# A reordered start of a second projection: the first two row tiles share the first column half, and two zeroings are moved

## The chip, the cores and the metric
The kernel runs on one core of one Trainium2 chip. The metric is the device time of one execution in microseconds, the median of several executions. The engines are TensorE (PE in the profile; its weight loads are PEld), VectorE (DVE), ScalarE (ACT), GpSimd (POOL) and SyncE (SP, which here only issues DMAs). Each engine works through its own program in order and meets the others through semaphores; a wait holds up everything behind it on that engine or DMA queue.

## The reference, cut to what matters
One layer of a hybrid decoder, on 2048 prompt tokens and 64 sample tokens (8 sequences of 8) of width 1024, in fp32:

```python
h = jnp.einsum('btd,de->bte', x, w_in)          # 1024 -> 4096, split in eight parts of 512
qa, ka, va, ga, qb, fb, ib, gb = jnp.split(h, IN_SPLITS, axis=-1)
# dilated window attention on qa, ka, va; gated linear recurrence on qb, fb, ib
# both gated by silu(ga), silu(gb), projected by w_out, then LayerNorm(alpha * x + z)
```

The change concerns `h` alone, and of it the columns of va, ib, ga and gb, which are wanted in natural layout (tokens on partitions). The sample tokens' recurrence, which takes the sample rows of ib, starts in the same stage.

## The kernel before, in words
`project_transposed` computes qa, ka, qb, fb with features on partitions and ends at some 380 us. `project_natural` follows: it computes the other four parts. Its rows are 17 tiles: 16 of 128 prompt tokens and one of the 64 sample tokens, `NTL = 17`. It goes through them twice, once for the columns of va and ib (the halves g = 0 and 1 of the first pass, 512 columns each), once for ga and gb. In the first pass `tile_of` puts the sample tile first: index j = 0 is the sample tile, j = 1 is tile 0, j = 2 tile 1, j = 3 tile 2, and so on. A **group** n is one tile by one half: before the change n = 2j + g throughout (`divmod(n, 2)`), 68 groups in all.

fp32 accuracy is had from two rounded parts: x = xhi + xlo and w = whi + wlo, and each group is 8 blocks of the contraction (k) times three products, 24 matmuls (L759, in `group`, L746) into a PSUM bank chosen by n % 2. `split_x(j)` on VectorE makes xhi by a cast (L487) and xlo by a subtraction (L489) into the buffer j % 2. The weights of one half are eight blocks: ScalarE rounds them (`round_w`, L661), VectorE subtracts (`split_w`, L494), counted by `w_split`, 8 per half. TensorE waits for these block by block only in the first tile of a pass (L756). `evacuate(n)` (L663 to 670) copies a group's bank into `stage[u]`, u = j % 2, counted by `evacuated`; `store(j)` on SyncE (L378) writes both halves of a tile to `projN` when both are evacuated; `load_x(j)` (L367) and `load_w` (L373) are on the same queue.

Between the groups stand other steps, placed by the group number n on every engine:
- After groups 0 and 1 TensorE makes seven pieces of the bias table (L838), six after group 0, one after group 1; each fp32 piece appears as two matmul records. VectorE copies them (L616) to `kf`. GpSimd, whose program begins with two zeroings (`at` L444, `qem` L445), waits for all seven copies and then spreads the table by DMAs (L447 to 461).
- The sample recurrence: at n = 2 VectorE and ScalarE compute the forget bounds and factors in turns (`bounds` L505, `decays` L672: an exponential at L674, the factors at L677 and L678). At n = 3 TensorE does levels 0 and 1 (L773), which need these factors; VectorE does `widen(0)`, `keep(0)`, `keep(1)` (L530 to 533, L503). After group 4 TensorE does level 2 (the third), which waits for `widen(0)` and `keep(0)`.

In VectorE's program the body of one n has first the split of x (`if n % 2`, the split of tile index j + 2, from L607), then the bias copies, then the recurrence's steps. That split has to wait until the last user of its buffer, tile index j, has both its groups done (L486). SyncE's program by n, up to n = 3, is: at n = 1 `store(0)`; at n = 2 a wait until that store has landed and the load of `v`, the sample rows of ib, from `projN` (L418, L419); at n = 3 `load_x(3)`, `store(1)`, then small loads for the attention. `load_x(2)` is issued ahead of the loop. ScalarE issues the load of the sample states, 2 MB, behind the evacuation of group 1 (L696).

Of the kernel before, what the change touches and what calls it, by code (L numbers as in the profile page):

```python
# [21 lines left out]
KD = D // P  # L22
# [257 lines left out]
def project_natural(nc, a, projT, projN, kwin_p, vwin_p, kwin_s, vwin_s, rep_p, rep_d, o_b, attn_s, state_out,  # L280
# [3 lines left out]
    NTL = T // P + 1  # L284
# [22 lines left out]
    def rows(j):  # L307
        return TS if tile_of(j) == NTL - 1 else P

    def attention_step(n):  # L310
        s, c = divmod(n - FIRST, EACH)
        return (s, c) if 0 <= s < NB else (None, None)

    with ExitStack() as ctx:
# [51 lines left out]
        def sync(sp):  # L366
            def load_x(j):  # L367
                n, u, t = rows(j), j % 2, tile_of(j) * P
                if j >= 2:
                    sp.wait_ge(x_split, j - 1)  # L370
                sp.dma_start(xraw[:, u, :, 0:n], a["xT"][:, :, t:t + n]).then_inc(x_landed[u], 16)

            def load_w(r, k):  # L373
                if r >= 1:
                    sp.wait_ge(w_split, KD * (r - 1) + k + 1)
                sp.dma_start(wraw[:, k], a["w_n"][:, k, r * H:(r + 1) * H]).then_inc(w_landed[k], 16)

            def store(j):  # L378
                n, u, t, c = rows(j), j % 2, tile_of(j) * P, j // NTL * 2 * H
                sp.wait_ge(evacuated, 2 * j + 2)  # L380
                sp.dma_start(projN[t:t + n, c:c + 2 * H], stage[0:n, u]).then_inc(stage_free[u], 16)

            def load_recurrence():
                for dst, src in ((lbp[:], a["lbT"]), (masks[:], a["smask"]), (rowm[:], a["rowm"]),
                                 (h_ident[:], a["ident"]), (q[:], projT[8:12, :, T:TT].rearrange("h p t -> p h t")),
                                 (sg[:], projT[12:16, :, T:TT].rearrange("h p t -> p h t"))):
                    sp.dma_start(dst, src).then_inc(h_landed, 16)

            def store_attention(s):
                sp.wait_ge(o_done, s + 1)  # L390
                for h in range(HA):
                    r, c = Q * (h // 2) + NT * (h % 2), DA * (h % 2)
                    sp.dma_start(attn_s[s * NT:(s + 1) * NT, h * DA:(h + 1) * DA],
                                 out[r:r + NT, s % 2, c:c + DA]).then_inc(out_free[s % 2], 16)

            sp.dma_start(exp_sb[:], a["expand"]).then_inc(b_landed, 16)
            sp.wait_ge(b_one, 1)
            sp.dma_start(table[0:BUCKETS, :], a["rel_bias"]).then_inc(b_landed, 16)
            for k in range(KD):
                load_w(1, k)  # L400
            load_x(2)
            for u in range(2):
                sp.wait_ge(stored_t[u], 16 * (NCT // 2 + 1))
            load_recurrence()
            for n in range(NGR):
                j = n // 2
                if n == 8:
                    for k in range(KD):
                        load_w(2, k)
                if n % 2:  # L410
                    if 2 < j + 2 < NTL * NPASS:
                        load_x(j + 2)
                    if j == NTL - 1:
                        for k in range(KD):
                            load_w(3, k)
                    store(j)
                if n == 2:
                    sp.wait_ge(stage_free[0], 16)  # L418
                    sp.dma_start(v[:], projN[T:TT, WB:2 * WB]).then_inc(hv_landed, 16)  # L419
                if n == HG:  # L420
                    sp.wait_ge(b_kept, 16)
                    sp.dma_start(ident[:], a["ident"]).then_inc(const, 16)
                    sp.dma_start(qs[:], projT[0:NG, :, T:TT].rearrange("g p t -> p g t")).then_inc(const, 16)
                    sp.dma_start(ks[:], projT[NG:2 * NG, :, T:TT].rearrange("g p t -> p g t")).then_inc(const, 16)
                if n == DELTA + 4:
                    sp.wait_ge(s_done, NB)
                    sp.dma_start(state_out.rearrange("b h k v -> k b h v"), S0[:]).then_inc(stored, 16)
                    sp.wait_ge(ho_out, 1)
                    sp.dma_start(o_b[T:TT, :], host[:]).then_inc(stored, 16)
                s, c = attention_step(n)  # L430
                if c == 4:
                    store_attention(s)
                if n == LAST + 1:
                    sp.wait_ge(qk_done, NB)
                    for dst, src in ((first["lmask"], a["lmask"]), (first["dmask"], a["dmask"]), (first["ident"], a["ident"])):
                        sp.dma_start(dst[:], src).then_inc(first["const"], 16)
                    for b in range(2):
                        load_segment(sp, projT, b, first["q"], first["sg"], first["qk_landed"])
            for u in range(2):
                sp.wait_ge(stage_free[u], 16 * (NTL - 1))  # L440
                sp.wait_ge(out_free[u], 16 * HA * NB // 2)

        def gpsimd(pool):
            nc.gpsimd.memset(at[:], 0.0).then_inc(mems, 1)  # L444
            nc.gpsimd.memset(qem[:], 0.0).then_inc(mems, 1)  # L445
            pool.wait_ge(b_copied, len(parts))
            pool.dma_start(vec_dram, vec).then_inc(b_kept, 16)  # L447
            pool.wait_ge(b_kept, 16)
            L = NC * LB
            pool.dma_start(rep_d, bass.AP(tensor=vec_dram.tensor, offset=L, ap=[[0, NT], [NV, HA], [1, LD]])  # L450
                           ).then_inc(b_repeated, 16)
            nc.gpsimd.memset(qb[:], 0.0).then_inc(zeroed, 1)
            nc.gpsimd.memset(bias[:], 0.0).then_inc(zeroed, 1)
            pool.wait_ge(zeroed, 2)
            pool.wait_ge(b_repeated, 16)
            for h in range(HA):
                r = Q * (h // 2) + NT * (h % 2)
                src = bass.AP(tensor=rep_d.tensor, offset=h * LD + NT - 1, ap=[[HA * LD - 1, NT], [1, WIN + NT]])
                pool.dma_start(bias[r:r + NT, :], src).then_inc(bias_landed, 16)
            pool.dma_start(rep_p, bass.AP(tensor=vec_dram.tensor, offset=0, ap=[[0, P], [NV, HA], [1, L]])  # L460
                           ).then_inc(b_repeated, 16)
            for u in range(2):
                pool.wait_ge(stored_t[u], 16 * (NCT // 2 + 1))
            for c in range(NG):
                pool.dma_start(kwin_p[c], projT[NG + c, :, 0:T]).then_inc(moved, 16)
                for b in range(NB):
                    pool.dma_start(kwin_s[b, c * P:(c + 1) * P, 1, WROWS - 1],
                                   projT[NG + c, :, T + b * NT:T + (b + 1) * NT]).then_inc(moved, 16)
            pool.wait_ge(stage_free[0], 16 * (NTL // 2 + 1))
            pool.wait_ge(stage_free[1], 16 * (NTL // 2))  # L470
            pool.dma_start(vwin_p, projN[0:T, 0:WA]).then_inc(v_out, 16)
            for b in range(NB):
                pool.dma_start(vwin_s[b, WIN - NT:WIN, :],
                               projN[T + b * NT:T + (b + 1) * NT, 0:WA]).then_inc(v_out, 16)
            pool.wait_ge(b_repeated, 32)
            pool.wait_ge(moved, 16 * NG * (NB + 1))
            pool.wait_ge(v_out, 16 * (NB + 1))

        def vector(dve):
            tt = nc.vector.tensor_tensor  # L480

            def split_x(j):
                n, u = rows(j), j % 2
                dve.wait_ge(x_landed[u], 16 * (j // 2 + 1))
                if j >= 2:
                    dve.wait_ge(group_done, 2 * j - 2)  # L486
                nc.vector.tensor_copy(xhi[:, u, :, 0:n], xraw[:, u, :, 0:n]).then_inc(x_hi, 1)  # L487
                dve.wait_ge(x_hi, j + 1)
                tt(xlo[:, u, :, 0:n], xraw[:, u, :, 0:n], xhi[:, u, :, 0:n].bitcast(F32), ALU.subtract).then_inc(x_split, 1)  # L489
# [154 lines left out]
        def scalar(act):  # L644
# [16 lines left out]
                nc.scalar.activation(whi[:, k, c], wraw[:, k], ACT.Copy).then_inc(w_hi, 1)  # L661

            def evacuate(n):  # L663
                j, g = divmod(n, 2)
                u, m = j % 2, rows(j)
                act.wait_ge(group_done, n + 1)
                if j >= 2 and g == 0:
# [76 lines left out]

        def tensor(pe):
            def group(n):  # L746
                j, g = divmod(n, 2)
                u, m, r = j % 2, rows(j), 2 * (j // NTL) + g
                if g == 0:
                    pe.wait_ge(x_split, j + 1)  # L750
# [2 lines left out]
                for k in range(KD):  # L753
                    if n >= NGR - 6:
                        first["early_scores"](pe, KD * (n - NGR + 6) + k)
                    if j % NTL == 0:  # L756
                        pe.wait_ge(w_split, KD * r + k + 1)
                    for b, (x, w) in enumerate(((xhi, whi), (xhi, wlo), (xlo, whi))):
                        mm = pe.matmul(acc[0:m, n % 2], x[:, u, k, 0:m], w[:, k, g * H:(g + 1) * H],  # L759
# [1280 lines left out]
```

## Time and profile before

| | us |
|---|---|
| runs shown, lowest / median / highest | 1552.85 / 1555.66 / 1557.06 |
| the profiled execution | 1562.63 |
| its span, first to last instruction | 1560.8 |
| TensorE busy | 1506.6 |
| VectorE, ScalarE, GpSimd busy | 768.2, 502.0, 440.1 |
| mean granted TensorE clock | 0.984 of full |

The profiled execution is 7.0 us longer than the median of the runs. A granted clock of 1.00 is 2.4 GHz, 0.50 is 1.2 GHz; a value between them is a stretch that holds some of each. Times in the trace are from the span's start. "Idle before" is how long the engine stood before an instruction, and the name behind it is what released it. The second projection begins at 382 us.

### The profile page before, as it was taken

What the parts mean: (1) busy time and instruction counts of PE and PEld (TensorE: products, weight loads), DVE (VectorE), ACT (ScalarE), POOL (GpSimd) and SP (SyncE); (2) the same over time, 40 slices, a digit from 0 to 9 for tenths busy, and PEclk for the clock granted to TensorE, in tenths of its full rate; (3) what the DMA queues carried; (4) which work ended last, traced back from release to release, by engine and by line L of the source; (5) the groups of instructions that cost most, each with busy time, mean ns of one, the idle gap of its engine ahead of it and who ended that gap; (6) DMA issues with size and microseconds to landing.
All of it is one profiled execution on the core that took longest, in us unless ns stands there. A gap on an engine that the chain in (4) does not pass through costs nothing.

```text
span 1560.8 us, 25524 instructions
## 1 busy us (share of the span) xinstructions
PE 1506.6 (97%) x9802; PEld 1348.0 (86%) x9802; DVE 768.2 (49%) x1941; ACT 502.0 (32%) x1426; POOL 440.1 (28%) x281
## 2 busy tenths in 40 slices
PE   7999999998999999989999999989899999999996
PEld 7999999997588777767778899989899999888885
DVE  6121120002423222222226699857677777898884
ACT  5111111112210113312222132357577777432231
POOL 0333210000150000100000100038797688344442
PEclk9999999999899999999999999999999999999998
DMA  9999998142694957967471399679698962966741
GB/s 302 332 325 345 340 330 243 41 143 91 187 326 146 325 194 248 334 230 253 154 253 48 79 290 339 199 231 200 153 195 194 195 166 77 315 209 206 221 158 54
DMA packets 174501, 338.34 MB, mean 217 GB/s; under 512 B 15635, under 2 KB 115283, under 8 KB 165523
## 3 DMA queue, kind: packets, MB, share of 16 engines
q1 hardware_dynamic: 141452, 169.18, 35.9%
q10 hardware_dynamic: 22432, 111.29, 22.1%
q0 software_dynamic: 10512, 56.48, 13.4%
q8 instruction: 65, 1.06, 0.3%
q14 instruction: 40, 0.33, 0.1%
HBM read 262.25 MB, written 155.39 MB: 268 GB/s over the span
## 4 chain that ended last, share of the span: by engine, by line
PE 63%; DVE 4%; DMA 4%; ACT 2%; issue 1%; POOL 1%; SPq 0%; DVEq 0%; ACTq 0%; POOLq 0%
PE banks L759 22%; PE banks L1878 11%; PE banks L1843 7%; PE banks L1815 5%; PE banks L1154 4%; PE banks L1829 4%; DMA spare<-in_xT 2%; PE banks L826 1%; DMA partials<-a_stage 1%; DVE at L1102 1%; PE banks L808 1%; PE banks L1859 1%; PE banks L1144 1%; DVE kf L1081 1%; PE banks L1199 1%
## 5 line engine op out<-in xcount | busy, mean ns | idle before, releaser
L256 PE MATMUL acc<-xhi,whi 128*128 128x424 f32 (+1 forms) x640 | 227.9, 356 | 8.7 <-DVE xlo L235 8.7
L759 PE MATMUL banks<-nwhi,nxhi 128*128 128x512 f32 (+1 forms) x544 | 220.6, 405 | 13.3 <-DVE nwlo L494 6.9
L256 PE MATMUL acc<-xlo,whi 128*128 128x424 f32 (+1 forms) x640 | 227.4, 355 | 0.0
L256 PE MATMUL acc<-xhi,wlo 128*128 128x424 f32 (+1 forms) x640 | 227.4, 355 | 0.0
L1453 POOL CAST a_sorted<-a_plain 128x2048 fp32r<-128x2048 f32 x45 | 171.1, 3856 | 167.0 <-DVE at L1102 132.9
L759 PE MATMUL banks<-nwhi,nxlo 128*128 128x512 f32 (+1 forms) x544 | 214.5, 394 | 0.0
L759 PE MATMUL banks<-nwlo,nxhi 128*128 128x512 f32 (+1 forms) x544 | 214.2, 394 | 0.0
L1718 ACT ACTIVATE a_prob<-a_prob,a_stage 128x256 f32<-128x256 f32 (+1 forms) x384 | 174.1, 454 | 80.0 <-DVE a_stage L1561 78.0
L1561 DVE CUSTOM_DVE_ANT_0 a_prob<-banks,a_bias 128x256 f32<-128x256 f32 (+1 forms) x384 | 125.2, 364 | 80.7 <-PE banks L1815 73.0
L1843 PE MATMUL banks<-a_v,a_probT 128*128 128x64 f32 x1200 | 157.7, 269 | 4.9 <-DVE a_probT L1573 4.9
L1843 PEld LDWEIGHTS banks<-a_v,a_probT 128*128 128x128 f32 x1200 | 150.0, 193 | 6.6 <-DVE a_probT L1573 6.0
L487 DVE CAST nxhi<-spare 128x1024 fp32r<-128x1024 f32 (+1 forms) x34 | 25.0, 736 | 252.5 <-DMA spare<-in_xT 171.7
L669 ACT ACTIVATE nstage<-banks 128x512 f32<-128x512 f32 (+1 forms) x68 | 40.6, 597 | 337.2 <-PE banks L759 337.2
L225 DVE CAST whi<-wraw 128x1024 fp32r<-128x1024 f32 x16 | 16.0, 1002 | 257.8 <-PE acc L256 166.1
L759 PEld LDWEIGHTS banks<-nwhi,nxhi 128*128 128x128 f32 (+1 forms) x544 | 101.5, 187 | 41.7 <-DVE nxlo L489 12.7
L275 ACT ACTIVATE stage<-acc 128x424 f32<-128x424 f32 (+1 forms) x80 | 41.6, 523 | 296.5 <-PE acc L256 296.3
L256 PEld LDWEIGHTS acc<-xhi,whi 128*128 128x128 f32 x640 | 121.4, 190 | 11.7 <-issue 7.9
L256 PEld LDWEIGHTS acc<-xhi,wlo 128*128 128x128 f32 x640 | 121.4, 190 | 2.2
L256 PEld LDWEIGHTS acc<-xlo,whi 128*128 128x128 f32 x640 | 121.4, 190 | 2.1
L759 PEld LDWEIGHTS banks<-nwhi,nxlo 128*128 128x128 f32 (+1 forms) x544 | 101.4, 186 | 24.6 <-issue 1.2
L759 PEld LDWEIGHTS banks<-nwlo,nxhi 128*128 128x128 f32 (+1 forms) x544 | 101.8, 187 | 21.4 <-issue 1.2
L1154 PEld LDWEIGHTS banks<-qd,kf 128*128 128x128 f32 x896 | 105.0, 192 | 6.4 <-issue 4.8
(212 smaller groups left out, 2537.1 us busy)
## 6 DMA issues: line engine op xcount, KB each, us to landing
a_plain<-split_qk POOLq DMA_DIRECT2D x48, 512.0 KB, 13.2
out_kwin_s<-in_cache_kT ACTq DMA_DIRECT2D x8, 2048.0 KB, 20.0
split_qk<-spare POOLq DMA_DIRECT2D x16, 1024.0 KB, 14.4
spare<-in_xT SPq DMA_DIRECT2D x32, 512.0 KB, 7.0
projN<-nstage SPq DMA_DIRECT2D x32, 512.0 KB, 5.5
qg<-in_cache_kT ACTq DMA_DIRECT2D x8, 2048.0 KB, 11.6
kf<-in_cache_v ACTq DMA_DIRECT2D x8, 2048.0 KB
out_kwin_s<-in_cache_kT ACTq DMA_DIRECT2D x8, 2032.0 KB, 29.7
```

The source lines that it names most:

```text
L256: mm = pe.matmul(acc[:, j, 0:n], w[:, u, k], x[:, k, c0:c0 + n], start=(k == 0 and a == 0), stop=(k == KD - 1 and a == 2))
L275: nc.scalar.activation(stage[:, u, c0:c0 + n], acc[:, j, 0:n], func).then_inc(bank_free, 1)
L669: nc.scalar.activation(stage[0:m, u, g * H:(g + 1) * H], acc[0:m, n % 2], ACT.Copy if j < NTL else ACT.Silu).then_inc(evacuated, 1)
L759: mm = pe.matmul(acc[0:m, n % 2], x[:, u, k, 0:m], w[:, k, g * H:(g + 1) * H], start=(k == 0 and b == 0), stop=(k == KD - 1 and b == 2))
L1154: mm = pe.matmul(a_ps[:, i % 3, a * CH // 2:(a + 1) * CH // 2].rearrange("p (n j) -> p n j", j=w), kd[u][:, h, t0:t0 + CH], late, start=Tr ...
L1453: nc.gpsimd.tensor_copy(dst[:, n].rearrange("p (r m) -> p r m", r=d), src[:, n].bitcast(F32).rearrange("p (m r) -> p r m", r=d)).then_inc( ...
L1561: ins = nc.vector.tensor_tensor_reduce(prob[:, n % 4, w, 2 * P - m:], s_ps[:, n % 3, w * 2 * P + 2 * P - m:(w + 1) * 2 * P], bias[g % 2][: ...
L1718: ins = nc.scalar.activation(pr, pr, ACT.Exp, bias=to[:, DA + 1:DA + 2], scale=-1.0, accum_out=to[:, DA:DA + 1])
L1815: mm = pe.matmul(s_ps[:, n % 3, w * 2 * P + (2 - m) * P:(w + 1) * 2 * P], source[:, 0, q0:q0 + P], source[:, 1 + a, k0:k0 + m * P], start= ...
L1829: mm = pe.transpose(t_ps[:, n % 3, a * P:(a + 1) * P], prob[:, n % 4, w, place * P:(place + 1) * P], ident[:])
L1843: mm = pe.matmul(o_ps[:, (n // 4) % 2, col:col + DA], probT[:, n % 3, a], v[g % 2][:, c, vt, x * DA:(x + 1) * DA], start=(a == 0 or ts[a - ...
L1878: mm = pe.matmul(z_ps[w][0:n, g], m[:, w, k, 0:n], ww[:, g * H:(g + 1) * H], start=(k == 0 and a == 0), stop=(k == KD - 1 and a == 2))
```

## The change
Two functions are added. `group_of(n)` gives the tile index and the half of group n: the first four are (0, 0), (1, 0), (0, 1), (1, 1) in place of (0, 0), (0, 1), (1, 0), (1, 1); all later ones stay. `both_done(j)` gives the count of groups after which tile index j has both halves: 3 for j = 0 (before: 2), and 2j + 2 for the rest as before. `store` and `split_x` wait for that count, `evacuate` and `group` take their tile and half from `group_of`, and TensorE's block-by-block wait for the weights' splits holds for the first four groups. GpSimd waits for all sixteen splits of the first two halves before its two zeroings.

```diff
+    def group_of(n):
+        return ((0, 0), (1, 0), (0, 1), (1, 1))[n] if n < 4 else divmod(n, 2)
+
+    def both_done(j):
+        return 3 if j == 0 else 2 * j + 2
...
             def store(j):
-                sp.wait_ge(evacuated, 2 * j + 2)
+                sp.wait_ge(evacuated, both_done(j))
...
         def gpsimd(pool):
+            pool.wait_ge(w_split, 2 * KD)
             nc.gpsimd.memset(at[:], 0.0).then_inc(mems, 1)
             nc.gpsimd.memset(qem[:], 0.0).then_inc(mems, 1)
...
                 if j >= 2:
-                    dve.wait_ge(group_done, 2 * j - 2)
+                    dve.wait_ge(group_done, both_done(j - 2))
...
             def evacuate(n):
-                j, g = divmod(n, 2)
+                j, g = group_of(n)
...
             def group(n):
-                j, g = divmod(n, 2)
+                j, g = group_of(n)
...
-                    if j % NTL == 0:
+                    if j % NTL == 0 or n < 4:
                         pe.wait_ge(w_split, KD * r + k + 1)
```

## Rows read from the trace of the kernel before

**Rows 1.** The page: busy time of each engine

```profile
PE 1506.6 (97%) x9802; PEld 1348.0 (86%) x9802; DVE 768.2 (49%) x1941; ACT 502.0 (32%) x1426; POOL 440.1 (28%) x281
```

**Rows 2.** Chain of waits: start us, duration us, engine, tile, line, count

```profile
385.82 7.04 PE banks L759 x24
392.86 7.66 PE banks L838 x12
400.52 8.11 PE banks L759 x24
408.97 5.70 PE banks L759 x24
...
643.78 26.14 DMA spare<-in_xT
...
671.95 7.35 PE banks L759 x24
```

**Rows 3.** Timeline of VectorE and GpSimd: start us, duration us, then instruction

```profile
382.09 2.26 DVE L487 CAST nxhi<-spare 128x512 fp32r<-128x512 f32 x1
382.27 1.80 POOL L445 MEMSET s_qem<- 128x2048 f32 x1
...
389.81 0.69 DVE L487 CAST nxhi<-spare 128x1024 fp32r<-128x1024 f32 x1
...
391.67 4.90 DVE L494 TENSOR_TENSOR nwlo<-spare,nwhi 128x512 fp32r<-128x512 f32 x8
```

**Rows 4.** Timeline of ScalarE behind the third group; in brackets idle before

```profile
414.69 0.60 ACT L669 ACTIVATE nstage<-banks 128x512 f32<-128x512 f32 x1 [5.43 <-PE banks L759]
...
416.60 0.21 ACT L674 ACTIVATE s_lbp<-s_lbp 128x8 f32<-128x8 f32 x1
```

**Rows 5.** Timeline of VectorE, 408 to 427 us

```profile
408.74 0.69 DVE L487 CAST nxhi<-spare 128x1024 fp32r<-128x1024 f32 x1 [7.50 <-PE banks L759]
...
411.00 0.17 DVE L509 TENSOR_TENSOR s_lbp<-s_lbp,bounds 128x8 f32<-128x8 f32 x1
...
423.24 0.69 DVE L487 CAST nxhi<-spare 128x1024 fp32r<-128x1024 f32 x1 [2.16 <-DMA spare<-in_xT]
...
425.85 0.98 DVE L503 COPY_PREDICATED s_at<-s_masks,banks 64x256 f32<-64x256 int32 x2
```

**Rows 6.** Timeline of TensorE: two levels, and its first matmul at 671.95

```profile
420.67 0.68 PE L773 MATMUL banks<-s_q,s_kd 128*64 128x64 f32 x8 [0.58 <-ACT s_fd L678]
...
427.44 0.68 PE L773 MATMUL banks<-s_qd,s_kd 128*64 128x64 f32 x8
...
671.95 0.80 PE L759 MATMUL banks<-nwhi,nxhi 128*128 128x512 f32 x1 [6.03 <-DVE nxlo L489]
```

**Rows 7.** Timeline of SyncE's queue

```profile
409.28 0.48 SPq L381 DMA_DIRECT2D projN<-nstage  x1
...
416.01 0.72 SPq L371 DMA_DIRECT2D spare<-in_xT  x1
```

**Rows 8.** DMA issues: at 409.3, 416.0, 423.6, 434.4, 434.8; last us to landing

```profile
projN<-nstage SPq DMA_DIRECT2D x1, 256.0 KB, 6.2
...
spare<-in_xT SPq DMA_DIRECT2D x1, 512.0 KB, 7.2
...
spare<-in_xT SPq DMA_DIRECT2D x1, 512.0 KB, 6.0
...
projN<-nstage SPq DMA_DIRECT2D x1, 512.0 KB, 10.0
...
spare<-in_xT SPq DMA_DIRECT2D x1, 512.0 KB, 24.6
```

**Rows 9.** Windows: busy of PE to POOL, granted clock, DMA share, GB/s

```profile
420.00:422.00 2.00, 1.42 (x18) 1.26 (x18) 0.42 (x1) 1.10 (x3) 1.43 (x1) 1.00 0.82 231
668.00:669.00 1.00, 0.00 (x0) 0.00 (x0) 0.00 (x0) 0.00 (x0) 0.00 (x0) 0.80 1.04 387
```

## The prediction

> **What bounds the kernel now.** I read the page's busy shares first: TensorE is busy 97% of a span of 1560.8 us [rows 1]. Time is gained only where TensorE waits or runs at its lower clock, and an added wait of TensorE lengthens the run. Then the chain of waits, because it shows what the start of this stage costs. The first group of 24 matmuls takes 7.04 us, then come twelve matmuls of the bias table in 7.66 us, then the second group in 8.11 us, and only the third has the full pace, 5.70 us [rows 2]. The chain starts from the first split of x on VectorE; the timeline there shows a cast of 512 columns taking 2.26 us, beside GpSimd's zeroing of 1.80 us, while a cast of 1024 columns without GpSimd takes 0.69 us [rows 3]. The second half's eight weight splits start at 391.67 us and take 4.90, so they are finished at 396.6 [rows 3]. The second group begins at 400.52 [rows 2]. So today no group waits for the second half: the bias matmuls cover it by some 4 us.
>
> **The zeroings, moved.** The first cast should take half of 0.69, so 0.35 us; that is 1.9 us less, and the low part, first weight split and TensorE follow it directly. ScalarE's first rounding, which the first weight split needs too, starts at the same moment as the cast and is over before the low part. TensorE starts at 383.9 instead of 385.82. In the sum the rest of the chain keeps its steps. The zeroings then run from about 394.7 (396.6 less 1.9), beside copies of bias products that nobody needs before the fourth group is over; GpSimd itself next waits for the last of these copies, so its queue loses nothing. The 1.9 us need not arrive whole. If the clock rises at the same moment as now, they were all spent at the lower clock, where a group's matmuls take about twice as long, and only 1.0 is left; if the bias matmuls and the second group come earlier to their own changes of clock, it can be up to 2.8 (the second group's excess over 5.70 is 2.4 us, the first's 1.3 [rows 2]). I take 1.9.
>
> **The order of the groups.** The same four groups of 24 matmuls are issued, so the work is equal. The new second group (tile 0, first half) needs x split 2, and that is made ahead of the second half's splits; the third group comes after some 400 us, when all sixteen splits are done. The order gains nothing: the 4 us of cover were there. I cost it at zero, and what hides the second half's splits stays the bias matmuls.
>
> **What the order delays.** The sample tile is now complete after the third group, not the second. Call the end of the third group G (414.69 now [rows 4], about 412.8 after). Two things hang on it.
>
> First, VectorE. It stands at the split of tile 1, which now waits for G, and behind it stand the last bias copy and the two operations of the forget bounds. Today that row of work starts at 408.74 and its last operation ends at 411.17, 2.43 us later [rows 5], long before ScalarE asks for it. After the change it ends at G + 2.5. ScalarE starts its exponential at G + 1.91 today (416.60 less 414.69 [rows 4]), then at G + 2.5. All the rest of that chain, to TensorE's first levels at 420.67 [rows 6], moves with it: 0.6 us more. TensorE idles there 0.58 us now, so 1.2 us after.
>
> Second, SyncE's queue, which is the larger. The store of the sample tile waits for both halves; behind it stand the reload of v, which waits for that store to land, and behind this the load of the x tile that the fourth split needs. Today the store is issued at 409.28 and the x load at 416.01 [rows 7], where its group ends at 408.63 (400.52 plus 8.11 [rows 2]). So the x load leaves 7.4 us behind the group that completes the tile: 6.2 us of landing of the store [rows 8] and the issues. After the change it leaves at G + 7.4, where today it left at G + 1.3. The x tile lands after 7.2 us in that place, or 6.0 us for the next one [rows 8]. Already now VectorE waits 2.16 us for it [rows 5], which is hidden. In VectorE's program the first widening and keeping of the sample levels stand behind that split; from the start of the cast (423.24) to the end of the first keeping (425.85 plus half of 0.98) are 3.1 us [rows 5]. TensorE needs that keeping for the third level, behind the fifth group.
>
> With 6.6 us for the transfer, the middle of 7.2 and 6.0, the third level can start at G + 7.4 + 6.6 + 3.1 = G + 17.1. Without the wait TensorE would be there at G + 12.75 (427.44 [rows 6] less 414.69) plus the 0.6 from above: G + 13.35. It stalls 3.8 us (3.75). The bounds are 2.0 (transfer 6.0, and store 1.2 quicker since the state's load is over sooner: taken as the difference of those two transfers) and 4.4 (transfer 7.2).
>
> **The clock behind that stall.** After a wait of 6.03 us [rows 6] TensorE's group took 7.35 us instead of 5.70 or so, and the granted clock fell within 668 to 669 us (0.80 there), some 2.8 us into the wait; at the wait of 0.58 us it stayed at 1.00 [rows 9]. A stall of 3.8 us lies above 2.8, so I take the fall. Its price lies between nothing and 1.65 us (7.35 less 5.70 [rows 2]); I take 1.5, the middle between that and the first group's 1.34 (7.04 less 5.70).
> The Trainium skill, TensorE: Matmul & The Clock Gate, section "HAM oscillation — how this bites in real kernels", says that a wait for DMA between tiles can send the engine back to 1.2 GHz so that the next tile starts cold. It speaks against this change: by it the sum is the one below, and without it 1.5 us less; the trace agrees for 6.03 us, and shows no wait between 0.58 and 6.03 here.
>
> **Sum.** −1.9 (zeroings) + 0.6 (levels) + 3.8 (third level) + 1.5 (clock) = +4.0 us. The profiled execution took 1562.63 us around its span of 1560.8, and would take 1566.6. It is 7.0 above the median of the runs, 1555.66, so against that the forecast is 1559.7. Later stages: the one long DMA wait in the chain, x at 643.78 for 26.14 us [rows 2], is for a load that is issued behind TensorE's own attention work, so it shifts along.
>
> **Rivals.**
> *The gain alone.* If x tile 2 lands so early that TensorE hardly stalls, −1.9 + 0.6 = −1.3 remains: 1554.4. The point is 3.8 us less of store and transfer than I reckoned. For it: the 2 MB state load is issued after the second group, which is over earlier relative to this store. Against it: the two waits stand in one queue, and the split was late already [rows 5]. Chance 0.22.
> *The late tile gets much later.* GpSimd's spread of the bias vector and the store of tile 1 (512 KB each) are issued close to the moved x load. A 512 KB store under such company took 10.0 us, and one x load 24.6 us [rows 8]. At 10.0 the stall grows by 3.4: +7.4, 1563.1; at 24.6 by 18.0: 1577.7. It decides the sign beyond doubt from a transfer of about 7.3 us on, where the sum passes +4.7. Chance 0.15.
> *The change does nothing that shows.* The second half was never waited for, and what moves early is taken up again where TensorE waits for DMAs anyhow (6.03 us at 671.95 [rows 6]): 1555.7. Against: that load is timed by TensorE's work. Chance 0.13.
> The forecast, a stall of 2 to 5 us, has 0.50.
>
> **How the numbers follow.** 0.3% of this kernel, about what a measurement can tell from no change, is 4.7 us. The forecast lies below that; with the bounds (gain 1.0 to 2.8, stall 2.0 to 4.4, clock 0 to 1.65) it runs from −0.2 to +5.7, and a quarter of its 0.50 is above +4.7. With most of the late-tile rival that makes slower 0.26. Faster by 4.7 needs more than all of the zeroings: 0.08, for what the profile does not show. Same 0.66. The range takes the gain alone at its best (−2.2) with 1 us of scatter at the lower end, and the 10.0 us transfer with 1 us at the upper: 1552.5 to 1564.
>
> **What would show it.** Right: the first cast at 0.35 us and TensorE's first matmul near 383.9; no TensorE wait for a weight split in the third or fourth group; VectorE's cast for x tile 2 waiting for its DMA until about G + 14; an idle of some 4 us of TensorE before the third level, behind VectorE's keeping, and a group after it of over 7 us at a granted clock of 0.5. Wrong: TensorE reaching the third level with no idle (then the gain alone), a cast still at over 2 us, or a stall of another group than the one behind the third level.

## The result, and the profile after

The changed kernel takes 1559.15 us (median of 10 runs, 1554.65 to 1563.16) against 1553.54 us for the kernel before (10 runs, 1549.27 to 1557.67). The ratio is 1.003, with a 95% interval from 1.0015 to 1.0044: slower by some 4.7 us by the ratio (5.6 between the medians), right at the bound that the prediction set between "the same" and "slower". The time lies in the forecast range, and the difference is the forecast +4.0 within its interval (2.3 to 6.8 us).

The profiled execution took 1560.87 us around a span of 1559.1. It can't be set whole against that of before, which took 1562.63, some 9 us above the median of its kernel's ten runs. So I compare the stage, not the span. From here on **T** is the distance from the stage's first instruction on VectorE (a small memset, at 382.08 us before and 380.55 after) to TensorE's first transpose of the sample keys, which stands behind group 6 (439.89 before, 442.32 after). T was 57.81 us before and is 61.77 after: **+3.96 us**, beside the +4.0 of the sum. That it agrees to a few hundredths is chance: the next section shows that T itself scatters by about 1 us.

The page's busy times of the changed kernel have hardly moved against [rows 1]:

```profile
PE 1504.6 (97%) x9802; PEld 1345.9 (86%) x9802; DVE 763.6 (49%) x1941; ACT 502.2 (32%) x1426; POOL 441.0 (28%) x281
```

The chain of waits of the changed kernel, with start, duration, engine, tile, line and count (L768 is the group's matmul, L847 the bias pieces, L782 the levels, L856 the transposes):

```profile
380.62 0.38 DVE nxhi L496
...
382.46 7.95 PE banks L768 x24
390.41 6.59 PE banks L847 x12
397.00 7.58 PE banks L768 x24
...
404.92 5.67 PE banks L768 x24
...
411.24 5.08 DMA projN<-nstage
...
416.84 8.29 DMA spare<-in_xT
...
425.16 0.70 DVE nxhi L496
...
428.33 1.09 PE banks L782 x8
429.42 6.79 PE banks L768 x24
436.20 0.61 PE banks L782 x8
436.81 5.67 PE banks L768 x24
442.48 0.44 PE banks L856 x4
```

Read it from the third group's end at 410.6. Before, the chain went from there to ScalarE's exponential and the levels [rows 2, 4]. Now it leaves the compute engines: the store of the sample tile (5.08 us to land), the reload of v, the load of x tile 2 (8.29 us), VectorE's split, the widening, the keeping, and only then TensorE. A chain that turns from PE to DMA in the middle of a stage is the sign of a new wait. The group behind that wait takes 6.79 us, its level 1.09; the next ones are back at 5.67 and 0.61.

TensorE's timeline after the change, with the idle before in brackets:

```profile
382.46 0.66 PE L768 MATMUL banks<-nwhi,nxhi 128*64 128x512 f32 x1 [4.23 <-DVE nwlo L503]
...
417.23 0.68 PE L782 MATMUL banks<-s_q,s_kd 128*64 128x64 f32 x8 [1.19 <-ACT s_fd L687]
...
428.33 1.09 PE L782 MATMUL banks<-s_qd,s_kd 128*64 128x64 f32 x8 [4.26 <-DVE s_at L512]
```

The first idle was 6.06 us before and is 4.23, the second 1.19 against 0.58 [rows 6], and the third, 4.26 us, is new. VectorE and SyncE's queue show why:

```profile
380.56 0.43 DVE L496 CAST nxhi<-spare 128x512 fp32r<-128x512 f32 x1
...
410.70 0.69 DVE L496 CAST nxhi<-spare 128x1024 fp32r<-128x1024 f32 x1 [12.98 <-PE banks L768]
...
425.16 0.69 DVE L496 CAST nxhi<-spare 128x1024 fp32r<-128x1024 f32 x1 [7.52 <-DMA spare<-in_xT]
```

```profile
411.24 0.48 SPq L389 DMA_DIRECT2D projN<-nstage  x1
416.34 0.46 SPq L427 DMA_DIRECT2D s_v<-projN  x1
416.84 0.60 SPq L379 DMA_DIRECT2D spare<-in_xT  x1
417.68 0.46 SPq L389 DMA_DIRECT2D projN<-nstage  x1
```

The first cast fell from 2.26 us [rows 3] to 0.43. The cast for x tile 2 waits 7.52 us for its DMA, where it waited 2.16 [rows 5], and the load left 6.2 us behind the third group's end instead of 1.3 [rows 7]. The granted clock fell behind the stall (windows: PE, PEld, DVE, ACT, POOL busy, then clock, DMA share, GB/s):

```profile
428.00:430.00 2.00, 1.67 (x10) 1.49 (x11) 1.13 (x5) 0.00 (x0) 1.32 (x2) 0.57 0.60 121
430.00:432.00 2.00, 2.00 (x7) 1.57 (x6) 0.59 (x2) 0.00 (x0) 0.00 (x0) 0.57 0.93 220
432.00:434.00 2.00, 2.00 (x10) 1.61 (x9) 0.00 (x0) 0.00 (x0) 1.21 (x3) 1.00 1.01 347
```

It fell in the stall or just behind it: the mean is already 0.57 from 428 to 430, where TensorE works again from 428.33, and it is back at 1.00 by 432.

### The profile page after: what moved, and what is told of

The parts are those of the page before. It is cut to its first block, busy times and chain, and to the rows that moved or that the text cites. A ratio compares the mean times of both kernels' runs of the same rounds, so it can differ in the third digit from the quotient of the medians.

```text
span 1559.1 us, 25526 instructions
## 1 busy us (share of the span) xinstructions
PE 1504.6 (97%) x9802; PEld 1345.9 (86%) x9802; DVE 763.6 (49%) x1941; ACT 502.2 (32%) x1426; POOL 441.0 (28%) x281
## 4 chain that ended last, share of the span: by engine, by line
PE 61%; DMA 5%; DVE 4%; ACT 2%; issue 1%; POOL 1%; SPq 1%; ACTq 0%; DVEq 0%; POOLq 0%
PE banks L768 22%; PE banks L1887 11%; PE banks L1852 7%; PE banks L1824 5%; PE banks L1838 4%; PE banks L1163 3%; DMA spare<-in_xT 2%; PE banks L835 1%; DMA partials<-a_stage 1%; DVE at L1111 1%; PE banks L817 1%; PE banks L1868 1%; DVE kf L1090 1%; DMA qg<-projT 1%; DVE qd L1089 1%
## 5 line engine op out<-in xcount | busy, mean ns | idle before, releaser
L768 PE MATMUL banks<-nwhi,nxhi 128*128 128x512 f32 (+1 forms) x544 | 221.6, 407 | 9.5 <-DVE nwlo L503 4.8
L768 PE MATMUL banks<-nwlo,nxhi 128*128 128x512 f32 (+1 forms) x544 | 215.4, 396 | 0.0
L768 PE MATMUL banks<-nwhi,nxlo 128*128 128x512 f32 (+1 forms) x544 | 215.3, 396 | 0.0
L225 DVE CAST whi<-wraw 128x1024 fp32r<-128x1024 f32 x16 | 12.3, 771 | 259.7 <-PE acc L256 213.3
L768 PEld LDWEIGHTS banks<-nwhi,nxhi 128*128 128x128 f32 (+1 forms) x544 | 102.3, 188 | 38.5 <-DVE nxlo L498 9.3
L768 PEld LDWEIGHTS banks<-nwhi,nxlo 128*128 128x128 f32 (+1 forms) x544 | 102.0, 188 | 24.7 <-issue 0.8
L768 PEld LDWEIGHTS banks<-nwlo,nxhi 128*128 128x128 f32 (+1 forms) x544 | 102.3, 188 | 21.3 <-issue 0.6
```

## The experiments

The runs are called e1 to e12. All are judged by T of their profiled execution, and those that were timed repeatedly by their ratio to the kernel before as well. The variants e5 to e8 have one timed run each (1558.40, 1552.28, 1555.46 and 1558.52 us, the kernel before 1554.28 beside them), which says little where the kernel before itself runs from 1549 to 1561 us.

T scatters too. From TensorE's first matmul of the stage to the end of the third group, the kernel before and the variants e8, e9, e11 and e12 issue the same matmuls in the same order with the zeroings at the head, and TensorE has no wait in between. This stretch took 28.85 us in the kernel before, 28.51 in e8, and 27.8 in the executions of e9, e11 and e12; only the stretches at the lower clock differ. So a difference of 1 us between the T of two executions needs no cause in the program. The idle times and the order of events inside one execution tell more.

**Theory:** SyncE's in-order queue makes the x tile late behind the landing of the sample tile's store, VectorE's in-order program passes that lateness to the sample levels, and the stall costs clock. **Rivals:** the moved zeroings shift GpSimd's DMAs; or VectorE's split of tile 1, held until the third group, is what costs; or the order gains what it was made for and loses elsewhere.

### One half of the change at a time

```diff
@@ zeroings alone, on the kernel before
+            pool.wait_ge(w_split, 2 * KD)
             nc.gpsimd.memset(at[:], 0.0).then_inc(mems, 1)
```

> The kernel before with the zeroings moved alone. The queue theory (SyncE's load of x tile 2 late behind the store of the sample tile, VectorE's steps late behind it): first cast about 0.4 us, TensorE's start some 1.9 us earlier in the stage, third group over some 2.5 us earlier, no idle before the third level; 2 to 3 us less than before, ratio about 0.998. The rival, that the moved zeroings shift GpSimd's later DMAs into dearer company and cost the time, expects it slower than before by some 4 us.

```diff
@@ order alone, on the changed kernel
-            pool.wait_ge(w_split, 2 * KD)
             nc.gpsimd.memset(at[:], 0.0).then_inc(mems, 1)
```

> The new order alone, zeroings at the head as before. Queue theory: first cast 2.26 us, TensorE idle 4 to 4.5 us before the third level, the fourth level reached some 6.5 us later in the stage than before; 6 to 6.5 us more than before, ratio about 1.004. The rival that the zeroings carry the loss expects no difference from before.

The zeroings alone: T = 54.61, 3.20 us less than before; the first cast took 0.43 us; ratio 0.999 (0.9978 to 1.0002). In the whole run the gain is not clear of noise; in the stage it is as expected. The order alone: T = 64.34, 6.53 us more; ratio 1.0042 (1.0026 to 1.0059), expected 1.004. TensorE's first and third level in that run, and the group behind the stall in its chain:

```profile
418.93 0.68 PE L781 MATMUL banks<-s_q,s_kd 128*64 128x64 f32 x8 [1.19 <-ACT s_fd L686]
...
430.07 1.08 PE L781 MATMUL banks<-s_qd,s_kd 128*64 128x64 f32 x8 [4.33 <-DVE s_at L511]
```

```profile
431.15 8.05 PE banks L767 x24
```

The same 1.19 and a stall of 4.33 us, with the zeroings at their old place. The whole loss comes with the order; the zeroings pay part of it back. The two halves add to +3.3 against the +3.96 of both together, which is within the scatter of T. The rival of the zeroings is out.

### Two ways to take the stall away, leaving the order

```diff
@@ e3: the load ahead of the reload of v
+                if n == 2:
+                    load_x(3)
                 if n % 2:
-                    if 2 < j + 2 < NTL * NPASS:
+                    if 3 < j + 2 < NTL * NPASS:
                         load_x(j + 2)
```

> The whole change, with the load of x tile 2 issued ahead of the reload of v instead of behind it. Queue theory: the x tile lands some 8 us after the third group, the idle before the third level goes to 0 and the clock stays up; about 5.5 us less than the change in the stage, 1 to 2 us less than before. The rival, that VectorE's split of tile 1, now behind the third group, is what costs, expects the stall to stay.

```diff
@@ e4: VectorE's program
-                if n % 2 and j + 2 < NTL * NPASS - 1:
+                if n % 2 and n != 3 and j + 2 < NTL * NPASS - 1:
                     split_x(j + 2)
...
                 if n == HG:
                     widen(0)
                     keep(0)
                     keep(1)
+                    split_x(3)
```

> The whole change, SyncE's queue as changed (late load), but VectorE does the first widening and both keepings ahead of the split of x tile 2. Queue theory: the x tile still lands late, VectorE still waits 4 us or more for it, but TensorE does not idle before the third level; same time as the variant with the early load within 1 us. If the late tile itself held TensorE, the idle would only move to the seventh group, about 4 us there.

Both bring it back. Early load: T = 56.10, 5.67 us less than the change, ratio 0.9993 (0.9978 to 1.0009). Split last: T = 55.85, ratio 0.9979 (0.9966 to 0.9991), faster than the kernel before by more than the scatter. In the second the tile is still late:

```profile
410.20 0.69 DVE L496 CAST nxhi<-spare 128x1024 fp32r<-128x1024 f32 x1 [12.92 <-PE banks L769]
...
423.76 0.69 DVE L496 CAST nxhi<-spare 128x1024 fp32r<-128x1024 f32 x1 [4.13 <-DMA spare<-in_xT]
```

VectorE waits 4.13 us for the DMA (expected 4 or more), and TensorE's third level starts with no idle before it:

```profile
416.74 0.68 PE L783 MATMUL banks<-s_q,s_kd 128*64 128x64 f32 x8 [1.19 <-ACT s_fd L688]
...
423.48 0.68 PE L783 MATMUL banks<-s_qd,s_kd 128*64 128x64 f32 x8
```

So the late tile by itself holds nobody; what stood behind its split in VectorE's program did. In both variants the split of tile 1 is still held until the third group, and its price is that TensorE idles 1.19 us before the first levels instead of 0.58, and no more. That rival is out too.

### The clock behind the stall

```diff
                 if HG < n < HG + NLV:
+                    if n == HG + 1:
+                        for _ in range(18):
+                            pe.matmul(bank[:, 2], xhi[:, 0, 0], whi[:, 0, 0:H], start=True, stop=True)
                     level(n - HG + 1)
```

> The whole change, with 18 extra 128x512 matmuls of no use between the fifth group and the third level (into a bank that is free there). Clock theory: the wait is still there but TensorE works through it, so the level and the group behind it run at full clock: the sixth group about 5.7 us instead of 6.8 and the levels 0.6 instead of 1.1, the fourth level 1.5 us earlier in the stage than with the change. If the idle and not the clock made that group long, it stays at 6.8.

T = 60.07, 1.7 us less than the change. The chain, with the filling matmuls at L854:

```profile
423.74 4.08 PE banks L854 x18
427.90 0.65 PE banks L782 x8
428.55 5.68 PE banks L768 x24
```

The level takes 0.65 us and the group 5.68, instead of 1.09 and 6.79. The level starts 47.6 us into the stage, in the change 47.8: the wait is as long, only the clock is kept. Its fall therefore cost 1.1 + 0.5 = 1.6 us in the change. That is not a fixed price. Behind the equal stall of the order alone (4.33 us) the group took 8.05 us and the level 1.08, so 2.8 us in all by the same count; the granted clock stood at 0.50 from 430 to 436 us there, while in the change it was back at 1.00 by 432.

### What the order is worth without its cover

```diff
-                if n in (0, 1):
+                if n in (1, 2):
                     pe.wait_ge(b_landed, 32)
-                    for m in range(6 * n, min(6 * n + 6, len(parts))):
+                    for m in range(6 * (n - 1), min(6 * n, len(parts))):
```

> Old order of the groups, zeroings moved, and the bias matmuls moved one group later (six behind the second group, one behind the third), so that nothing stands between the first and second group. If the bias matmuls were what hid the second half's splits, TensorE now waits at the second group; by the splits' own pace (0.61 us each, 0.7 us of matmuls a block) the waits sum to under 1 us. If the order is worth what it was made for, several us of waits.

> The same move of the bias matmuls with the new order of the groups. No wait for a weight split in the first four groups under any theory; the difference to the old order's run up to the second group is what the order can be worth at most: under 1 us by my theory. The stall before the third level is there as in the change, 3 to 5 us.

Old order, then new order, both with the zeroings moved:

```profile
382.33 13.87 PE banks L760 x48
396.21 5.24 PE banks L839 x12
401.45 7.29 PE banks L760 x24
```

```profile
382.45 12.40 PE banks L768 x48
394.85 6.41 PE banks L847 x12
401.26 7.71 PE banks L768 x24
```

Without the bias pieces in between, the first two groups take 13.87 us in the old order and 12.40 in the new. That is not the order's worth. Between 382.3 us and the bias pieces TensorE waits for nothing in either execution, and the second group starts 5.6 us ahead of their start in the old order and 5.5 in the new. The difference lies in the first group, which is the same 24 matmuls in both: 8.2 us against 6.8, because the lower clock lasted longer. The windows from 386 to 388 us, old order first, then new (granted clock 0.50 and 1.00):

```profile
386.00:388.00 2.00, 2.00 (x6) 0.98 (x6) 1.97 (x3) 0.96 (x2) 0.00 (x0) 0.50 0.99 339
```

```profile
386.00:388.00 2.00, 2.00 (x10) 1.21 (x9) 1.97 (x3) 0.64 (x2) 0.00 (x0) 1.00 1.01 343
```

A second execution of the old-order kernel (e10 below) needed 12.82 us for the same two groups. So even without its cover the order earns some 0.1 us: the second half's first split is done 1.7 us (0.7 in e10) before the second group starts. "Under 1", as I expected, was right.

The third group ends as early in one as in the other (28.36 and 28.45 us into the stage), because the bias pieces and the third group then ran longer at the lower clock with the new order (6.41 + 7.71 us against 5.24 + 7.29). My expectation for the new order was wrong on the stall: it isn't there (T = 54.30, beside 53.55 in the old order). The second group ends some 10 us earlier in the stage than in the change, ScalarE's load of the states leaves earlier with it, and the store of the sample tile then lands in 2.9 us instead of 5.1 and the x tile in 5.6 instead of 8.3. So the size of the stall follows how fast these two transfers land; that the load of the states is what sped them up is likely and was not tested.

### The queue alone, in the old order

```diff
@@ e8: the reload of v waits, on the kernel before
                 if n == 2:
+                    sp.wait_ge(evacuated, 3)
                     sp.wait_ge(stage_free[0], 16)
```

> The kernel before with one wait added on SyncE: the reload of v, and with it the load of x tile 2, also waits until the third group is evacuated. Order of groups, VectorE's program and zeroings are as before. Queue theory: the x tile leaves about 0.7 us behind the third group instead of 1.3, no later than before in effect, since the store has landed by then: no stall, time unchanged within 1 us. It separates the wait for the third group as such (harmless) from the landing of the store behind it.

T = 57.50 against 57.81: nothing lost. The store landed as the third group was evacuated, and the x load left 33.4 us into the stage, before 33.9. The wait for the third group as such costs nothing; the store's landing behind it does.

```diff
@@ e9, e12: the store waits, on the kernel before
             def store(j):
-                sp.wait_ge(evacuated, 2 * j + 2)
+                sp.wait_ge(evacuated, 3 if j == 0 else 2 * j + 2)
```

> The kernel before, old order and old zeroings, with one number changed: the store of the sample tile waits for three evacuations instead of two, as it must in the new order. Queue theory: this alone brings the stall. The store leaves 0.7 us behind the third group, lands 5 to 6 us later, the x tile of the fourth split leaves at the third group + 6.5 and TensorE idles about 4 us before the third level; the fourth level 5 to 6.5 us later in the stage than before, the run 5 to 6 us longer (ratio about 1.0035). If the order of the groups or VectorE's split of tile 1 is what costs, no stall and no difference.

> A second look at the late store alone, for another profiled execution of a kernel whose runs spread from 1556 to 1575 us. Queue theory: TensorE's idle before the third level is 1.6 us or more, up to 5; where the total is long, the added time is TensorE's idle behind splits of x tiles 2 and 3 in this stage. If both idles are as small as in the first look and the total is long, the loss is somewhere else in the kernel.

One number, in an otherwise unchanged kernel, and it is slower than the whole change: 1.0072 (1.0045 to 1.0099), with runs from 1556 to 1575 us. In the first profiled execution, at 1556.14 us the shortest of its runs, T was only 59.17, and the idle before the third level 1.62 us, not the 4 that I expected. The second took 1570.66 us, and there T is 67.54. Its TensorE:

```profile
429.89 0.65 PE L773 MATMUL banks<-s_qd,s_kd 128*64 128x64 f32 x8 [3.20 <-DVE s_at L503]
...
449.86 1.06 PE L847 MATMUL banks<-s_ident,s_kd 128*64 128x128 f32 x4 [5.76 <-DVE s_fd L533]
```

and the chain of the second idle:

```profile
424.58 22.51 DMA spare<-in_xT
...
447.12 0.78 DVE nxhi L487
...
449.86 1.06 PE banks L847 x4
```

The first idle, 3.20 us, is the predicted one. It follows the landing of x tile 2: 5.2 us for an idle of 1.62, 6.7 for 3.20, and 8.3 for the 4.26 of the change. The second, 5.76 us, is the same mechanism one tile on: the load of x tile 3 needed 22.5 us, and VectorE's last widening stands behind its split. The queue alone is enough for a stall. T is 9.7 us longer than before, and the end, counted from the stage's start, 7.9, so the loss of this execution against the profiled one of before lies here. Against the median of the kernel before on the same chip (1555.45) it is 15 us longer, and of that T explains about 10.

```diff
@@ e11: e9 and e4's move of the split together
```

> The late store of the run before this, in the old order, with VectorE's first widening and keepings ahead of the split of x tile 2. The late store alone cost 0.7% with a wide spread, though its profiled execution idled only 1.6 us before the third level and 0.6 later, behind a load of x tile 3 that took 14.7 us. If that loss is all at the third level through VectorE's order, this variant comes back to the kernel before, ratio 0.999 to 1.001. If it lies in the loads behind (x tile 3 and on, which this edit doesn't help), it stays at 1.004 or more with the wide spread.

Ratio 1.0054 (1.0031 to 1.0077), still widely spread. The third level has no idle now, but T is 65.43, because of this:

```profile
446.11 1.06 PE L848 MATMUL banks<-s_ident,s_kd 128*64 128x128 f32 x4 [8.50 <-DVE s_fd L533]
```

The wait of 8.50 us stands behind x tile 3, whose load took 20.4 us here. So in the old order, as far as these executions show, most of the loss lies at tile 3, which the edit did not help. Why that load took 14.7 and 22.5 us in the two executions of e9, 10.6 in the changed kernel and 6.0 before [rows 8], is not settled. In e9 and e11 it leaves within 5 us of the load of tile 2 and the store of tile 1, in the kernel before 7.6 us behind the former, but in the changed kernel it left within 4 us of both and took 10.6; how far ahead of GpSimd's large copies it leaves (5.8 and 8.9 us in e9's two executions, 12.3 in the changed kernel, 7.9 before) does not put them in order. Nothing was run to tell these apart.

### The version that beats both

```diff
@@ e10: on the kernel before
+            pool.wait_ge(w_split, 2 * KD)
             nc.gpsimd.memset(at[:], 0.0).then_inc(mems, 1)
...
-                if n in (0, 1):
+                if n in (1, 2):
                     pe.wait_ge(b_landed, 32)
-                    for m in range(6 * n, min(6 * n + 6, len(parts))):
+                    for m in range(6 * (n - 1), min(6 * n, len(parts))):
```

> The old order with the zeroings moved and the bias matmuls one group later, as in the single look before, now timed. In that look the sample levels were over 4.2 us earlier in the stage than before, with 1.5 us of them spent in the second group on the second half's splits. Expected 3.5 to 4.5 us less than before, ratio about 0.997, and so the fastest of the variants; if what is won here is given back at later DMA waits, the ratio stays within 0.999 to 1.001.

Old order, zeroings moved, bias pieces one group later (the same kernel as in the look at the old order above): T = 52.46 here and 53.55 there, 5.35 and 4.26 us less than before, where I expected 3.5 to 4.5; ratio 0.9971 (0.9959 to 0.9984), so 1552.42 us beside 1556.17 for the kernel before on the same chip. The first groups in its chain:

```profile
383.55 12.82 PE banks L760 x48
396.37 5.24 PE banks L839 x12
401.62 7.26 PE banks L760 x24
```

It has the lowest ratio of the variants, but the split-last variant (0.9979, 0.9966 to 0.9991) is not told apart from it. The expectation says that 1.5 us of the second group went on waits for the second half's splits; the traces show no such wait in either execution.

## Why the prediction was right

- **The zeroings.** Taken at −1.9 for the start; measured 1.83 (first idle 4.23 for 6.06). The Trainium skill, SBUF — State Buffer, section "Who interferes with whom", says that VectorE in a two-port mode and GpSimd contend, and that whoever issues first holds the other up for its whole instruction; the 2.26 us beside the 0.30 and 1.80 us of zeroing, and 0.43 without, agree. By the third group's end the gain was 2.5 us (32.61 to 30.07 us into the stage), inside the bound of 2.8. Most of the growth is the scatter of the clock: the other executions with the old head (e8, e9, e11, e12) end that group 31.5 to 32.2 us into the stage, those that start as the change does (the changed kernel, e3, e4, e5) 30.0 to 30.2, so the gain lies between 1.3 and 2.6 us, with 1.8 as the mean.
- **The order gains nothing.** Right: in the changed kernel no group waits for a weight split, and in the kernel before none did [rows 2, 3]. The reason was half right: the prediction says that the bias matmuls hide the second half's splits, but with these moved away (e6, e10) TensorE still waits for none of them.
- **The first levels.** Idle of 1.2 us forecast, 1.19 measured, behind VectorE's bounds.
- **The queue and the stall.** Right in place, in kind and nearly in size: 3.8 us forecast, 4.26 measured. The terms: store 6.2 us taken, 5.1 measured; x tile 6.6 taken, 8.3 measured. Both were mis-sized, in opposite directions, and so the sum of both was off by only 0.6. The prediction took the middle of two transfers of before; here the store of tile 1 left 0.8 us behind the load, where before it left 5.1 us behind, which may be why it took longer.
- **The clock.** 1.5 forecast, 1.6 measured and isolated by the filling matmuls. The agreement is partly luck: the forecast priced the group alone, which lost 1.1 us (6.79, not the "over 7" of the signs), and left out the level, which lost 0.5. And behind the equal stall of the order alone the price was 2.8 us, above the forecast's bound of 1.65.
- **The sum.** −2.5 + 0.6 + 4.3 + 1.6 = +4.0 measured in the stage, against −1.9 + 0.6 + 3.8 + 1.5 = +4.0 forecast. The mechanism is the predicted one; that the sum agrees this closely is luck. In these two executions the gain and the stall were each half a us too small, and with the mean gain of 1.8 us the same terms give +4.7, the measured difference by the ratio.
- **The chances.** "The same" was the likeliest, at 0.66; the result stands on its bound. The rival of the much later tile did not come true in the change, but the late store in the old order shows that it was a real one: 22.5 us for the load of x tile 3, and +0.7%. The 24.6 us that it was built on say little, though: they belong to the load of x tile 4, and that took 21.8 to 25.1 us in every execution of this document.
- **Open.** The profiled executions don't show the +3.96 at their ends (1178.7 us from the stage's start before, 1178.5 after). Most of it is carried on at first: the first matmul of line L1144 (by the lines of the kernel before) comes 445.4 us into the stage before and 448.2 after, and in all executions of this document it follows the end of T by 385.5 to 388.7 us. What the execution of before lost, it lost behind that point. One idle there, at L1144, is 2.1 us before and 0.7 after; the rest was not traced.

## What to carry to other kernels

When work is reordered on one engine, list what each other queue has standing behind the step that becomes complete later: here a 256 KB store held a reload, which held a load, which held a split, which held four small operations that TensorE needed. Reorder for a wait only if the trace shows that wait; here there was none, with the bias pieces between the groups or without. Moving the zeroings and the bias pieces made the kernel faster (ratio 0.9971), moving the groups made it slower. And put the small operations that others wait for ahead of a large one that waits for a DMA.

## What was unexpected of the hardware

The same idle can cost clock or not. In the changed kernel TensorE's first matmul of the stage comes after an idle of 4.23 us and took 0.66 us, at the lower clock (its line stands in the section on the result). In e10, after 4.22 us, the first four took some 0.4 us, at the full clock, and the fall came later:

```profile
383.55 0.41 PE L760 MATMUL banks<-nwhi,nxhi 128*64 128x512 f32 x1 [4.22 <-DVE nwlo L495]
383.81 0.39 PE L760 MATMUL banks<-nwlo,nxhi 128*64 128x512 f32 x1
...
385.22 0.63 PE L760 MATMUL banks<-nwhi,nxhi 128*64 128x512 f32 x1
```

So a stall's clock price has scatter of its own, over a us here (12.82 us for the first two groups in that run, 13.87 in the other look at the same kernel, and 1.6 against 2.8 us behind the two equal stalls before the third level). A gain of 1 us that is read from one trace each of two kernels can be nothing else, as the 1.5 us of the look without the bias pieces were. Second, over the fourteen executions the 512 KB load of x tile 2 landed after 5.2 to 8.3 us, and that of x tile 3 after 6.0 to 22.5; a few us of slack behind such a load are not safe.
